# One block for the output projection and both MLP halves of a hybrid layer

## The reference

```python
mix_l = y @ w_o + b_o            # y: gated sum of the two branches
xl = layernorm(ALPHA * xl + mod_l[2] * mix_l, g1, b1p)
h  = xl * (1 + mod_l[4]) + mod_l[3]
m  = square(relu(h @ w1 + b1)) @ w2 + b2      # w1 1024 x 4096, w2 4096 x 1024
xl = layernorm(ALPHA * xl + mod_l[5] * m, g2, b2p)
```

## Time and profile before

| | us |
|---|---|
| median of 3 runs | 3507.51 (3505.79 to 3512.71) |
| the profiled execution | 3508.18 |
| its span | 3506.5 |
| TensorE busy | 3177.1 (91%) |
| VectorE busy | 1855.3 (53%) |
| ScalarE busy | 599.9 (17%) |
| mean granted clock of TensorE, of full speed | 0.957 |

### The profile page before, as it was taken

The page is one execution under the profiler, slowest core; times in us unless marked ns, Lnnn a source line. Parts: engine busy times, 40 slices in busy tenths (PEclk is TensorE's granted clock), DMA queues, the critical chain, the costliest instruction groups (busy, mean ns, idle before and its releaser), DMA issues. The chain is left out here.

```text
span 3506.5 us, 37636 instructions
## 1 busy us (share of the span) xinstructions
PE 3177.1 (91%) x14552; PEld 2571.5 (73%) x14552; DVE 1855.3 (53%) x2529; ACT 599.9 (17%) x1032; POOL 277.3 (8%) x415
## 2 busy tenths in 40 slices
PE   5999999999997899569799599999999599999997
PEld 3878888888874788447577488888887488888885
DVE  3831132122216788387576665555556665555556
ACT  2421000111114555311000211111110211111110
POOL 0322010000002111100000000000000000000000
PEclk8999999999998999879899799999999799999998
DMA  5632243333316433446544411111111321111111
GB/s 208 217 119 78 74 119 101 106 118 120 117 70 212 122 101 114 153 149 200 148 141 134 144 54 48 48 48 47 45 46 42 132 66 47 45 45 45 45 48 48
DMA packets 244198, 347.84 MB, mean 99 GB/s; under 512 B 14947, under 2 KB 162675, under 8 KB 242550
## 3 DMA queue, kind: packets, MB, share of 16 engines
q1 hardware_dynamic: 196806, 201.54, 18.6%
q0 software_dynamic: 32864, 109.09, 8.8%
q10 hardware_dynamic: 14416, 35.65, 3.0%
HBM read 248.18 MB, written 98.05 MB: 99 GB/s over the span
## 5 line engine op out<-in xcount | busy, mean ns | idle before, releaser
L137 PE MATMUL mlp_bank<-mlp_h2h,mlp_w1h 128*128 128x512 f32 x1024 | 407.1, 398 | 23.3 <-ACT mlp_a L1878 23.3
L1845 DVE TENSOR_TENSOR mlp_acc<-mlp_acc,mlp_bank 128x512 f32<-128x512 f32 x480 | 321.7, 685 | 175.6 <-PE mlp_bank L139 175.6
L137 PE MATMUL mlp_bank<-mlp_w2h,mlp_ah 128*128 128x512 f32 x1024 | 402.9, 393 | 9.9 <-DVE mlp_acc L1798 9.9
L137 PE MATMUL head_bank<-head_hTh,head_wh 128*128 128x512 f32 x1024 | 407.6, 398 | 2.9 <-DVE head_hTl L549 2.0
L139 PE MATMUL mlp_bank<-mlp_h2h,mlp_w1l 128*128 128x512 f32 x1024 | 406.3, 397 | 0.0
L138 PE MATMUL mlp_bank<-mlp_h2l,mlp_w1h 128*128 128x512 f32 x1024 | 406.1, 397 | 0.0
L138 PE MATMUL head_bank<-head_hTl,head_wh 128*128 128x512 f32 x1024 | 405.3, 396 | 0.0
L139 PE MATMUL head_bank<-head_hTh,head_wl 128*128 128x512 f32 x1024 | 405.2, 396 | 0.0
L139 PE MATMUL mlp_bank<-mlp_w2h,mlp_al 128*128 128x512 f32 x1024 | 401.4, 392 | 0.0
L138 PE MATMUL mlp_bank<-mlp_w2l,mlp_ah 128*128 128x512 f32 x1024 | 400.9, 391 | 0.0
L557 DVE CAST head_wh<-head_raw 128x1024 fp32r<-128x1024 f32 x64 | 44.6, 696 | 584.7 <-PE head_bank L139 433.5
(11 more groups left out here) (228 smaller groups left out, 4681.2 us busy)
## 6 DMA issues: line engine op xcount, KB each, us to landing
mlp_raw<-in_w SPq DMA_DIRECT2D x128, 512.0 KB, 4.0
head_raw<-in_w_in SPq DMA_DIRECT2D x64, 512.0 KB, 4.1
scratch_proj<-head_stage POOLq DMA_DIRECT2D x128, 256.0 KB, 2.7
head_x<-in_w_ada ACTq DMA_DIRECT2D x8, 2048.0 KB, 10.0
merge_gates<-scratch_proj SPq DMA_DIRECT2D x32, 512.0 KB, 5.2
head_wa<-in_w_ada SPq DMA_DIRECT2D x8, 1024.0 KB, 5.9
mix_dec<-scratch_proj SPq DMA_DIRECT2D x32, 256.0 KB, 4.1
scratch_dft_a<-mix_fa POOLq DMA_DIRECT2D x32, 256.0 KB, 4.0
```

Source lines behind the costliest of these rows:

```text
L137: nc.tensor.matmul(out, wh, xh, start=(k == 0), stop=False)
L1845: nc.vector.tensor_tensor(dst, dst, V[n % 4][:], ALU.add).then_inc(acc_s, 1)
```

## The change

`phase_out_proj` and the two calls of `phase_mlp` become one block, `phase_tail`, without a register loop. Its buffers are laid over each other by hand (`place`). The engines' lists are:

- The projection works on 16 tiles of 128 rows. The second half's rows come first (`row0`). The first two tiles follow the weight strips together, and so do the last two; the last two release the places of `wo` to the MLP's weights (`k_used`).
- The high part of y is cast by ScalarE, the low part made by VectorE, one tile at a time.
- The rows of a tile are loaded into `acc`, scaled, summed and normalized in place. There is no `xo`.
- The tiles of the second half are stored to `xn1`, transposed and split into `hT` between projections (`turned`), and their h2 is stored to two new scratch tensors `h1h` and `h1l` of type fp32r. The places in `acc` are then loaded for the first half's tiles. These stay in `acc`, and their h2 stays in `hT`.
- The first half's transposes stand between projections, in the last two tiles, and between up pieces 0, 1 and 2, 3 of the first pair.
- Between the halves GpSimd reads h2 back into `hT` once the last up of the first half has ended (8.4 MB in two transfers). It reads each tile of rows back into `acc` once the tile's result has been stored. The second half's first up stands right behind the first half's last down in TensorE's list, and `residual(1, ...)` behind its hidden pieces in VectorE's.
- g2 and b2p are loaded into `raw2`, after `split2` of the next pair. The second half's first `w2` strips after that wait until all results of the first half are out.

The core of the diff (the removed blocks are the functions printed above):

```diff
+        acc = place("acc", [P, NT, D], 0)
+        hT = place("h2h", [P, KD, HW], 32, F32R), place("h2l", [P, KD, HW], 64, F32R)
...
+        def row0(j):
+            return (j * P + HW) % T
+        def turned(j):
+            m = j % 4 - 1
+            return j // 4 - 1, 3 * m, min(3 * m + 3, KD)
...
+            def load_x(j):
+                if j >= 4:
+                    sp.wait_ge(z_s, j - 3)
+                if j >= NT:
+                    sp.wait_ge(st_r[j - NT], 16)
+                    sp.wait_ge(xT, KD * ((j - NT) // 4 + 1))
+                sp.dma_start(acc[:, j % NT], d["xn"][row0(j):row0(j) + P, :]).then_inc(ld_x[j % 4], 16)
...
+            for j in range(2, NTILE):
+                load_y(j)
+                if j + 2 < NT:
+                    load_x(j + 2)
+                if j > NT:
+                    load_x(j - 1)
...
+                if q % NQ == 0 and q or q == 2 * NQ - 1:
+                    sp.wait_ge(w2lo, 2 * q + 2)
+                    for n, src in enumerate(("g2", "b2p")):
+                        sp.dma_start(raw2[:, n, :], d[src].partition_broadcast(P)).then_inc(ld_t, 16)
...
+            dve.wait_ge(st_res, 16)
+            low_y(2)
+            for j in range(NTILE):
+                if 3 <= j + 2 < NTILE:
+                    low_y(j + 2)
+                rows_of_tile(j)
+                if 5 <= j < NTILE - 2 and j % 4:
+                    split_h(*turned(j))
+                if j == NTILE - 3:
+                    split1(0)
+                    split_h(2, 3, KD)
+            hidden(0, (0, 1))
+            split_h(3, 0, KD)
+            split2(0)
+            hidden(0, (2,))
+            split1(1, (0,))
+            hidden(0, (3,))
+            split1(1, (1,))
+            residual(0, 0)
+            residual(0, 1)
+            split2(1)
+            for x, q in order():
+                if x == "u":
+                    if q % NQ:
+                        hidden(q)
+                    elif q:
+                        hidden(q, (2, 3))
+                        split1(q + 1, (1,))
+                        residual(1, 0)
+                        residual(1, 1)
+                        split2(q + 1)
+                elif q % NQ == NQ - 1:
+                    gather_rows(q)
+                else:
+                    gather(q)
+                    if q + 2 < 2 * NQ:
+                        split2(q + 2)
...
+            two_tiles(NTILE - 2)
+            up(0, (0, 1))
+            transposes(3, 0, KD)
+            up(0, (2, 3))
+            for x, q in order():
+                if x == "u" and q:
+                    up(q)
+                elif x == "d":
+                    down(q)
...
+                    pool.wait_ge(up_s, 4 * NQ)
+                    for s in range(2):
+                        pool.wait_ge(st_h[s], 32)
+                    for n, src in enumerate(("h1h", "h1l")):
+                        pool.dma_start(hT[n][:], d[src]).then_inc(ld_h, 16)
                 for t in range(NT):
+                    pool.wait_ge(out_s, NT * h + t + 1)
+                    pool.dma_start(d["out"][h * HW + t * P:h * HW + (t + 1) * P, :], acc[:, t]).then_inc(st_out[t], 16)
+                if h == 0:
+                    for t in range(NT):
+                        pool.wait_ge(st_out[t], 16)
+                        pool.dma_start(acc[:, t], d["xn1"][HW + t * P:HW + (t + 1) * P, :]).then_inc(ld_a[t % 4], 16)
```

More of the change, by code:

```diff
@@ L1625, in _ @@
             step.up(nc.vector.scalar_tensor_tensor(resv[:, 1, :], resv[:, 1, :], ALPHA, resv[:, 2, :], ALU.mult, ALU.add))
+            dve.wait_ge(ld_v, 48)
+            step.up(nc.vector.tensor_scalar(ag[:], ag[:], ALPHA, None, ALU.mult))
             step.wait(dve)
[L1627 to L1631 removed]
@@ L1632, in _ @@
-            i = NB // 2 - 1
-            split(i, 1)
-            for q in range(2):
-                for t in range(2):
-                    tile(i, q, t)
+            dve.wait_ge(st_res, 16)
[9 more added lines that the diff above has]
+                    split_h(2, 3, KD)
@@ new lines, in _ @@
+            for j in range(3):
+                high_y(j)
+            for j in range(NTILE):
+                if 3 <= j + 2 < NTILE:
+                    high_y(j + 2)
+                if 5 <= j < NTILE - 2 and j % 4:
+                    gi, lo, hi = turned(j)
+                    evict_h(gi, lo, lo + 2)
+                    root(j)
+                    evict_h(gi, lo + 2, hi)
+                else:
+                    root(j)
+                if j == NTILE - 3:
+                    evict_h(2, 3, KD)
@@ L1668, in _, with project @@
-            blk(0, 1)
-            with pe.Fori(1, NB // 2) as i:
-                for q in range(2):
-                    blk(i, q)
+            def project(j, k, c):
+                out, cs = bank[2 * (j % 3) + c][:], slice(c * 512, (c + 1) * 512)
+                nc.tensor.matmul(out, ys[:, j % 3, 0, k], wo[:, k, 0, cs], start=(k == 0), stop=False)
+                nc.tensor.matmul(out, ys[:, j % 3, 0, k], wo[:, k, 1, cs], start=False, stop=False)
+                return nc.tensor.matmul(out, ys[:, j % 3, 1, k], wo[:, k, 0, cs], start=False, stop=(k == KD - 1))
@@ new lines, in _ @@
+            two_tiles(0)
+            for j in range(2, NTILE - 2):
+                pe.wait_ge(yl_s, j + 1)
+                for c in range(2):
+                    free(j, c)
+                    for k in range(KD):
+                        last = project(j, k, c)
+                    last.then_inc(mm_s, 1)
+                if j >= 5 and j % 4:
+                    transposes(*turned(j))
+            two_tiles(NTILE - 2)
+            up(0, (0, 1))
+            transposes(3, 0, KD)
+            up(0, (2, 3))
@@ L2004, in build_program @@
         phase_merge(nc, d, g)
-        phase_out_proj(nc, d, g)
-        for half in range(2):
-            phase_mlp(nc, d, g, half)
+        phase_tail(nc, d, g)
 def shape_constants():
```

669 lines of the change are left out of this document (328 added, 341 removed).

## The result

| | before | after |
|---|---|---|
| median of 4 runs each, us | 3506.65 (3503.87 to 3512.71) | 3456.14 (3455.89 to 3457.75) |
| the profiled execution, us | 3508.18 | 3455.89 |
| its span, us | 3506.5 | 3454.1 |
| TensorE, VectorE, ScalarE busy, us | 3177.1, 1855.3, 599.9 | 3150.6, 1842.5, 615.4 |
| mean granted clock | 0.957 | 0.961 |

The ratio of the medians is 0.9855, 95% interval 0.9838 to 0.9872. The change saves 50.5 us; the forecast was 34.9 (3473.3 us). TensorE is busy 26.5 us less, although the change takes out no product and no transpose (96 in the projection stage and 32 behind it, where 64 stood at each seam): a part of the gain is not idle time that went away.

What follows compares the result with a forecast made beforehand. It took the steady part as bound by TensorE's matmuls, with gains only where TensorE isn't fed: 13.8 us before the first `down` plus 21.1 between halves, 3508.2 - 34.9 = 3473.3 us; 3460 to 3490 at 0.75, outer range 3456 to 3500.

Steps and rivals of the forecast that it cites:

- a pitch of the projection 0.007 us longer: Sign against the forecast: output projection matmuls further apart than the assumed 0.2266 us, 4.5 us in all.
- Start of the projection: First pair of output projection tiles: ends at 1778.9 as before, give or take 2; nothing gained or lost.
- Projection: Output projection with its added transposes: ends at 1959.8, 11.8 later than before, including 3.3 us of wait for `split1(0)`.
- First hole: First half's first `down`, after its fourth group: TensorE waits about 11 us for VectorE's queue.
- VectorE's wait for the second half of `res`: Between the residual additions: the second half of `res` comes only after the first is used up, 4.3 us.
- Second seam: Between the MLP halves, from the last addition of `gather(14)` to the second half's first `down`: 21.1 us saved.
- norm vectors: Second seam: last norm's gain and bias, asked for only after `split2(16)`, make `gather_rows` wait 5.3 us.
- wait for the rows: Second seam: VectorE waits 11 us for the second half's rows, there at 39.5 (36.5 to 48).
- The slower one: Rival: second half's h2 read-back between fp32r tensors lands late, at 65 GB/s 67 us past its window, 3540 us; chance 0.09.
- VectorE eats it: Rival of no change: turned projection tiles run 2 to 3 us over TensorE and rows come late, 3503 us; chance 0.05.
- More gained: Rival: shortest transposes, no wait at `split1(0)`, norm vectors in time, rows at 36.5; 3458 us or a little under; chance 0.08.
- The rule of the skill against it: GpSimd can't write DMA descriptors during VectorE's two-port casts, so the rows' reload would wait; 2 us more.

Runs made afterwards that it cites:

- e1: The kernel before with 288 unused bytes per partition ahead of `raw1`, so `w1h` and `h2h` start at the same remainder modulo 512: 3485.99 us against 3506.00.
- e2: The kernel after with buffers from place 96 on moved 224 bytes, so `w1h` and `h2h` are as far apart as before: 3479.11 us.
- e5: The kernel after with 80 unused floats per partition ahead of the input projection's transposed rows, aligning them with its weights modulo 256: 3437.25 us, 18.9 less than after.
- e6: The kernel after with only VectorE's work at the two seams put in another order: 3442.38 us, 13.8 less than after.
- e4: Matmuls alone, no layer: 24 cases of 144, starts of weights and columns offset by various bytes; 226.7 to 234.3 ns from matmul to matmul.
- e10: Matmuls alone, 14 cases of 144, each pass on its own line, high and low operands offset separately; 226.7 to 236.4 ns from matmul to matmul.
- e7: The kernel after with the second half's rows read back one tile behind each store, not all behind the eighth: 3454.05 us, 2.1 less than after.
- e9: The kernel after with 14 of GpSimd's 16 final waits put ahead of the last store's issue: 3455.24 us in one run.
- e11: The kernel after with the edits of e5, e6 and e7 together, plus the edit of e9: 3416.03 us.
- e12: The kernel after with the edits of e5, e6 and e7, its semaphores reordered to clear in four contiguous ranges, not five: 3417.68 us.

## Why the prediction was wrong, and what of it held

The direction and the work at the seams held; the size missed by 15.6 us, and one step carries all of that and more.

*The step that failed:* "So the steady part is bound by its matmuls, which the change keeps, and only the places where TensorE is not fed can give anything", and again "TensorE's 560 us without a hole came from a loop, so there is nothing to win". TensorE was busy 560 of 560 us at full clock, and yet each up matmul took a step of 0.2333 us where 0.2266 is to be had. Busy time and granted clock both read full either way. So a term for the matmuls themselves was put at nothing. It is worth 3072 x 0.0067 = 20.6 us; e1 measures it as 20.0 in the kernel before, e2 as 23.0 in the kernel after, or 18.9 in the part of the program that the edit touches. The hint stood in the trace of before: two groups of the same shape, 398 ns (up) and 393 (down), and a pitch of 0.2266 that I read off the projection and never held against the up phases. I even named "a pitch of the projection 0.007 us longer" among what would make the prediction wrong; a difference of that size came, but in another stage and with the other sign.

*Without that step* the change is worth 50.5 - 20.6 = 29.9 us. Measured with the fast step in both kernels, from e1 to after, it is 3485.99 - 3456.14 = 29.9; with the slow step in both, from before to e2, 3506.00 - 3479.11 = 26.9. (Only the second pair was measured side by side; between occasions the median of before moved from 3505.9 to 3508.2.) The forecast for that part was 34.9, so its own terms were 5 to 8 us too large. Its terms, from the two profiled executions:

- Until the end of the stages ahead of the projection, 4.3 us less in the trace of after. The code there is the same, and executions of before alone range from 3498.9 to 3512.7: not a gain of the change. It makes 52.4 of the two spans' difference into 48.1.
- *Start of the projection:* as before, forecast give or take 2: 7.8 us idle at 1781.07 against 6.8 at 1785.75.
- *Projection:* its end forecast for 1959.8, less the 4.3 us 1955.5; it came at 1957.9. The wait for `split1(0)`, forecast 3.3, shows as 3.4 at 1949.31.
- *First hole:* forecast 11, measured 10.8. VectorE's wait for the second half of `res`, forecast 4.3, measured 4.6. From the end of the merge to the last addition of `gather(14)` the trace is 22.4 us shorter, and the step of 14 up phases, 96 x 0.0067 us each, takes 9.0 of it: 13.4 for the seam, forecast 13.8.
- *Second seam:* norm vectors forecast 5.3, measured 5.9; wait for `res` 4.3 and 4.4; wait for the rows 11 and 15.0; hole 24 and 27.7. The rows' wait, sized from two loads of 2 MB, is the term that was too small: three weight loads and the last store run beside the rows, twelve transfers of 512 KB, and from 2724 to 2736 the DMA engines move 389 to 410 GB/s at a share of 1.02 to 1.04. From the last addition of `gather(14)` to the first addition of the last `gather_rows` 28.9 us less, again with 9.0 of the step: 19.9, forecast 21.1.
- *The end:* forecast as unchanged ("The end of the kernel has the same `gather_rows`, and it doesn't change"), measured 3.2 us longer (5.3 to 8.5). The additions are the same; what follows the last store is not: GpSimd's DRAIN at the end of the block takes 3.88 us and not 1.03. The blocks of before that the change takes out had such DRAINs in the seams, 1.60 and 1.03 us.

13.4 + 19.9 - 3.2 = 30.1, and 48.1 - 18.0 is the same. This takes off the step of 28 up phases; with that of the four inside the seams too, it is 27.5. A slip in the forecast's list, eight splits of 1.06 us counted as 9.5 and not 8.5, changes nothing, since TensorE's pieces end that stretch.

*The rivals.* The slower one, the late read-back of h2, fell clearly: its 8.4 MB were issued at 2635.2 and the last byte landed at most 22.8 us after its issue (the trace's longest landing for `h2l`), where 61 us were to be had before the first up matmul at 2696.5. 8.4 MB in 23.3 us are 360 GB/s, against the 65 that I weighed it with and the 49 and 159 of the rows that I took it from the earlier trace rows. So a DMA between two fp32r tensors is no slow path here. *VectorE eats it* fell too: the turned tiles cost TensorE 1.7, 0.4, 0.4, 0.4, 0.7 and 0.4 us, all by waits for ScalarE. *More gained* had the right time (3458, "or a little under") by luck: the norm vectors were not in time, and the rows were later and not earlier.

*The rule of the skill against it.* Two casts of VectorE (starts 2721.20 and 2722.27, 0.42 and 0.69 us) lie beside the seven issues of rows from 2721.05 on, which took 4.10 us together, 0.4 more than 7 x 0.53. The two issues that they fall into took 0.70 and 0.82 us, and each ends 0.12 us after its cast. The Trainium skill, "SBUF — State Buffer", section "SBUF: two separate sides", would have the issues wait for the casts, by my estimate 2 us in all; the trace agrees that they wait, but only an issue that meets a cast does, and the price here is 0.4 us.

## What to carry to other kernels

Before calling a stretch bound by TensorE's matmuls, compare the step from start to start between stages whose matmuls have one shape: a busy share of 100% at full clock hid a difference of 3% here. When a change moves tiles in SBUF, compare the addresses of the matmul operands too, and put weights and columns (and their low parts) at the same remainder modulo 256; it costs a pad of a few hundred bytes, and here it was worth 20 us in the up phases (e1) and 19 in the input projection (e5), with 3072 matmuls each. And where a barrier is taken out, look at which engine's list is now the longest: here it was VectorE's, and putting work into the waits of that list gave 14 us (e6).

## What the runs showed of the hardware that was not expected

- A matmul of 128 by 512 in fp32r, with new weights each time, follows the one before it after 226.7 to 227.0 ns when both operands start at the same address modulo 256, and after 233.2 to 234.3 at most other distances, at full clock and with all other engines idle (e4). The longest steps were 235.5 with high weights and low columns 96 off, and 236.4 with all columns 240 off (e10). The Trainium skill, "SBUF — State Buffer", section "Operand start alignment", allows any start at a multiple of the element's size and says that this is about legality, not speed; the speed is what these runs add.
- A read-back of 8.4 MB in two DMAs between fp32r tensors took 23.3 us, beside the steady traffic of the weights; from 2640 to 2650 the DMA engines moved 418 GB/s in all, at a share of 0.99.
- A store of 512 KB lands in 2.9 us as a median, and with a load of the same size issued 0.5 us behind it still in 2.9 to 4.7 (six of e7). The one that met three weight loads and full DMA engines took 7.7 (e7), in the kernel after 6.5.
- The DRAIN with which GpSimd ends a block took 1.03 us behind 12 of its DMAs and 3.88 behind 47. Neither fewer waits (e9, e11) nor fewer ranges of semaphores to clear (e12) changed it.
